# Token-shift mixing moved from the loaded RWKV blocks to the point where each projected block leaves PSUM

## What is computed

```python
shifted = jnp.pad(p_in, ((0, 0), (1, 0), (0, 0)))[:, :-1]
xl = p_in + (shifted - p_in) * mu
r, k, v, xw, xa, xg = jnp.split(xl, RWKV_SPLITS, axis=-1)
```

## Time and profile before

| | us |
|---|---|
| median of 3 runs | 2064.92 |
| lowest, highest | 2062.79, 2067.34 |
| profiled execution | 2061.17 |
| its span | 2059.4 |
| TensorE busy in the span | 1906.2 (93%) |
| VectorE busy | 859.3 (42%) |
| ScalarE busy | 426.5 (21%) |
| GpSimd busy | 1278.9 (62%) |

### The profile page before, as it was taken

How to read it: one execution, slowest core, us unless ns; L and a number is a source line. 1 busy time by engine, 2 the same in 40 slices (tenths; PEclk the granted TensorE clock), 3 DMA queues, 4 the chain that set the end, 5 groups by cost and what they waited for, 6 DMA issues and landing times.

```text
span 2059.4 us, 29817 instructions
## 1 busy us (share of the span) xinstructions
PE 1906.2 (93%) x11700; PEld 1482.6 (72%) x11700; DVE 859.3 (42%) x1426; ACT 426.5 (21%) x862; POOL 1278.9 (62%) x619
## 2 busy tenths in 40 slices
PE   7999999888779999999799989997868799999998
PEld 5888888656557888888477866676755678888887
DVE  4333321267664333311404244357756635555301
ACT  3000000123431000000213145534431021111100
POOL 6888877734066888877375442333364667777773
PEclk9999999989989999999899999999968999999999
DMA  4222223311022222233242421140023222223231
GB/s 149 92 92 98 93 86 94 118 35 59 11 82 72 92 92 93 92 96 97 99 160 98 160 100 53 42 149 8 4 109 112 72 82 92 92 92 93 91 95 59
DMA packets 58780, 180.33 MB, mean 88 GB/s; under 512 B 6931, under 2 KB 13843, under 8 KB 58172
## 3 DMA queue, kind: packets, MB, share of 16 engines
q1 hardware_dynamic: 49132, 165.83, 24.0%
q10 hardware_dynamic: 9552, 13.13, 1.8%
HBM read 165.81 MB, written 13.13 MB: 87 GB/s over the span
## 4 chain that ended last, share of the span: by engine, by line
PE 82%; DVE 12%; ACT 3%; issue 2%; DMA 0%; ACTq 0%; POOL 0%; DVEq 0%; SPq 0%; POOLq 0%
PE bank L531 23%; PE bank L533 23%; PE bank L532 23%; PE bank L893 1%; DVE h_lo L1643 1%; PE bank L846 1%; PE bank L581 1%; PE bank L879 1%; DVE xT L1690 1%; DVE tmp L1687 1%; DVE sq L2205 1%; PE bank L810 1%; DVE m_lo L2206 1%; DVE sq L2202 1%; PE bank L1051 1%
## 5 line engine op out<-in xcount | busy, mean ns | idle before, releaser
L444 POOL TENSOR_TENSOR w_hi<-w_raw,one 128x1024 fp32r<-128x1024 f32 (+1 forms) x279 | 527.1, 1889 | 595.1 <-PE bank L533 584.0
L446 POOL TENSOR_TENSOR w_lo<-w_raw,w_hi 128x1024 fp32r<-128x1024 f32 (+1 forms) x279 | 696.4, 2496 | 21.9
L531 PE MATMUL bank<-h_hi,w_hi 128*128 128x512 f32 x1528 | 628.1, 411 | 26.6 <-DVE h_lo L1643 12.5
L532 PE MATMUL bank<-h_lo,w_hi 128*128 128x512 f32 x1528 | 606.8, 397 | 0.0
L533 PE MATMUL bank<-h_hi,w_lo 128*128 128x512 f32 x1528 | 606.5, 397 | 0.0
L531 PEld LDWEIGHTS bank<-h_hi,w_hi 128*128 128x128 f32 x1528 | 288.8, 189 | 119.5 <-issue 27.9
L532 PEld LDWEIGHTS bank<-h_lo,w_hi 128*128 128x128 f32 x1528 | 289.3, 189 | 76.0 <-issue 9.8
L533 PEld LDWEIGHTS bank<-h_hi,w_lo 128*128 128x128 f32 x1528 | 288.8, 189 | 70.5
L531 PE MATMUL bank<-a_hi,w_hi 128*128 128x512 f32 x528 | 208.6, 395 | 0.0
L532 PE MATMUL bank<-a_lo,w_hi 128*128 128x512 f32 x528 | 208.6, 395 | 0.0
L533 PE MATMUL bank<-a_hi,w_lo 128*128 128x512 f32 x528 | 208.6, 395 | 0.0
(11 more groups left out here) (342 smaller groups left out, 2116.0 us busy)
## 6 DMA issues: line engine op xcount, KB each, us to landing
w_raw<-w_ffn_gu_dram SPq DMA_DIRECT2D x88, 512.0 KB, 3.4
w_raw<-w_conv_up_dram SPq DMA_DIRECT2D x44, 512.0 KB, 3.5
w_raw<-w_ffn_down_dram SPq DMA_DIRECT2D x32, 448.0 KB, 3.2
w_raw<-w_ffn_down_dram SPq DMA_DIRECT2D x16, 512.0 KB, 3.5
w_raw<-w_out_dram SPq DMA_DIRECT2D x16, 512.0 KB, 3.5
w_raw<-w_gates_dram SPq DMA_DIRECT2D x16, 512.0 KB, 3.5
w_raw<-w_rwkv_dram SPq DMA_DIRECT2D x14, 512.0 KB, 3.4
w_raw<-w_conv_down_dram SPq DMA_DIRECT2D x16, 448.0 KB, 3.3
```

The costliest lines, as they stand in the source:

```text
L444: nc.gpsimd.tensor_tensor(w_hi[:, s, 0:width], raw, one[:, 0:1].to_broadcast([P, width]), ALU.mult).then_inc(sem("w_rounded"), 1)
L446: nc.gpsimd.tensor_tensor(w_lo[:, s, 0:width], raw, w_hi[:, s, 0:width].bitcast(F32), ALU.subtract).then_inc(sem("w_split"), 1)
L531: nc.tensor.matmul(dst, hi, rhs_hi[:, k, :], start=start and k == k0, stop=False)
L532: nc.tensor.matmul(dst, hi, rhs_lo[:, k, :], start=False, stop=False)
```

## The change

The mix moves to where a block leaves PSUM. For each of the 14 RWKV blocks:

- ScalarE's copy now multiplies by 1 - mu, a column of the new tile `stay`, that VectorE makes once.
- VectorE then adds mu times the block shifted by one token, read from the same bank, in one instruction over 511 tokens (`mix_shifted`). Only this one now returns the bank to TensorE (`fill_read`).
- ScalarE's DMA of block f is issued by `send(f)` at the start of block f + 1's turn, after a wait for VectorE.
- The 14 `mix_shifted` stand at fixed places in VectorE's order in the attention's preparation: one behind each head's scaling, one more, two behind the four kd products, and six around the two compressions; the last stands ahead of the first attention unit's masks.
- `mix` and its 14 calls are gone. Readers of `pin` wait for the load alone.

The blocks in DRAM are now mixed ones. Nothing else changes.

```diff
--- before.py
+++ after.py
@@ -163,6 +163,7 @@
         head_ones2, eye2 = rcs[:, 6 * C:6 * C + P], rcs[:, 6 * C + P:]
         w2a2 = sb("w2a2", [P, 4 * P])
         PC = sb("PC", [P, 4, NCH])
+        stay = sb("stay", [P, 14])
         keep = sb("keep", [P, 4])
         psum = ctx.enter_context(nc.psum_tensor("bank", [P, 8, S], F32))
         bank = [psum[:, i, :] for i in range(8)]
@@ -1372,9 +1373,19 @@
             logs()
             filled = [0]
 
+            def send(f):
+
+                late = f - NFILL + LATE
+                act.wait_ge(*nth("fill_read", f + 1))
+                act.dma_start(fill_dram.ap()[:, f * S:(f + 1) * S],
+                              stage[:, f % 8, :] if late < 0 else late_stage[:, late, :])\
+                    .then_inc(sem("fill_late" if late >= 0 else f"fill_out{f // 4 % 2}"), 16)
+
             def fill_out(n=1):
 
                 for f in range(filled[0], filled[0] + n):
+                    if 1 <= f <= 14:
+                        send(f - 1)
                     act.wait_ge(*nth("w_used", FIRST["rwkv"] + f + 1))
                     late = f - NFILL + LATE
                     if f == 0:
@@ -1382,10 +1393,16 @@
                     elif f >= 8 and f % 4 == 0 and late < 0:
                         act.wait_ge(*nth(f"fill_out{f // 4 % 2}", 64 * (f // 8)))
                     place = stage[:, f % 8, :] if late < 0 else late_stage[:, late, :]
-                    nc.scalar.activation(place, bank[fill_bank(f)][:, :], ACT.Copy).then_inc(sem("fill_read"), 1)
-                    act.wait_ge(*nth("fill_read", f + 1))
-                    act.dma_start(fill_dram.ap()[:, f * S:(f + 1) * S], place)\
-                        .then_inc(sem("fill_late" if late >= 0 else f"fill_out{f // 4 % 2}"), 16)
+                    if f < 14:
+
+                        if f == 0:
+                            act.wait_ge(*nth("stay_ready", 1))
+                        c = RW_ORDER[f]
+                        nc.scalar.activation(place, bank[fill_bank(f)][:, :], ACT.Copy, scale=stay[:, c:c + 1])\
+                            .then_inc(sem("fill_scaled"), 1)
+                    else:
+                        nc.scalar.activation(place, bank[fill_bank(f)][:, :], ACT.Copy).then_inc(sem("fill_read"), 1)
+                        send(f)
                 filled[0] += n
 
 
@@ -1495,7 +1512,7 @@
                 act.wait_ge(*nth("keep_ready", 1))
                 nc.scalar.activation(MOD[:, :], RATE[m], ACT.Identity, bias=keep[:, m:m + 1], scale=param("k_a", m))\
                     .then_inc(sem("key_rate"), 1)
-                act.wait_ge(*nth("mixed_in", 3 * m + 5))
+                act.wait_ge(*nth(f"pin_in{m + 1}", 16))
                 if m:
                     act.wait_ge(*nth("rw_head_sum", 2 * m - 1))
                 nc.scalar.activation(sq[:, 0, :], pin[:, 4 + m, :], ACT.Square, scale=param("k_k", m))\
@@ -1518,7 +1535,7 @@
                     .then_inc(sem("kk_rstd"), 1)
 
             fill_out(2)
-            act.wait_ge(*nth("mixed_in", 2))
+            act.wait_ge(*nth("pin_in0", 16))
             nc.scalar.activation(pin[:, 13, :], pin[:, 13, :], ACT.Sigmoid)
             nc.scalar.activation(pin[0:64, 12, :], pin[0:64, 12, :], ACT.Tanh).then_inc(sem("lora_in"), 1)
             fill_out(1)
@@ -1876,6 +1893,15 @@
             pre_norm("nsa", "attn_norm", "nsa_h_ready")
             dve.wait_ge(*nth("nsa_small_in", 8 * 16))
             nc.vector.memset(rel[32:33, :], 1.0).then_inc(sem("rel_one"), 1)
+            nc.vector.tensor_scalar(stay[:, :], prm[:, COL["mu"]:COL["mu"] + 14], -1.0, 1.0, ALU.mult, ALU.add)\
+                .then_inc(sem("stay_ready"), 1)
+
+            def mix_shifted(f):
+
+                place, c = stage[:, f % 8, :], RW_ORDER[f]
+                dve.wait_ge(*nth("fill_scaled", f + 1))
+                nc.vector.scalar_tensor_tensor(place[:, 1:], bank[fill_bank(f)][:, 0:S - 1], param("mu", c),
+                                               place[:, 1:], ALU.mult, ALU.add).then_inc(sem("fill_read"), 1)
             job = [0]
 
             def job_bank():
@@ -1910,15 +1936,21 @@
                 dve.wait_ge(*nth("head_rstd", i + 1))
                 nc.vector.tensor_tensor(zn[:, i, :], zn[:, i, :], tmp[:, i, :], ALU.mult)\
                     .then_inc(sem("head_rstd_used"), 1)
+                if i:
+                    mix_shifted(i - 1)
             for i in range(2, 6):
                 dve.wait_ge(*nth("head_rstd", i + 1))
                 nc.vector.scalar_tensor_tensor(reverse(qn[:, i - 2, :]), by_tile(zn[:, i + 4, :]), param("q_norm"),
                                                by_tile(tmp[:, i % 2, :]),
                                                ALU.mult, ALU.mult).then_inc(sem("head_rstd_used"), 1)
+                mix_shifted(i - 1)
+            mix_shifted(5)
             for c in range(4):
 
                 nc.vector.tensor_scalar(kd[:, c, :], job_bank()[:, :], param("k_norm"), -HD ** -0.5, ALU.mult,
                                         ALU.mult).then_inc(sem("nsa_read"), 1)
+            mix_shifted(6)
+            mix_shifted(7)
             chain = [0]
 
             def link(ins):
@@ -1936,6 +1968,9 @@
                 link(nc.vector.tensor_tensor(t, x, x, ALU.mult))
                 link(nc.vector.scalar_tensor_tensor(t, t, 0.044715, x, ALU.mult, ALU.mult))
                 nc.vector.tensor_tensor(t, t, x, ALU.add).then_inc(sem("gelu_arg"), 1)
+                mix_shifted(8 if v == 0 else 11)
+                if v == 0:
+                    mix_shifted(9)
                 dve.wait_ge(*nth("gelu_tanh", v + 1))
                 link(nc.vector.scalar_tensor_tensor(t, t, 1.0, x, ALU.add, ALU.mult))
                 nc.vector.tensor_scalar(x, t, 0.5, None, ALU.mult).then_inc(sem("gelu"), 1)
@@ -1946,9 +1981,12 @@
                     link(nc.vector.tensor_tensor(kcn[:, :], kcn[:, :], tmp[:, 0, 0:w], ALU.mult))
                     nc.vector.tensor_scalar(kcn[:, :], kcn[:, :], param("k_norm"), -HD ** -0.5, ALU.mult, ALU.mult)\
                         .then_inc(sem("kc_normed"), 1)
+                    mix_shifted(10)
                 else:
                     nc.vector.tensor_copy(vct[:, :, :].rearrange("n g d -> n (g d)"), job_bank()[0:NCMP, 0:2 * HD])\
                         .then_inc(sem("nsa_read"), 1)
+                    mix_shifted(12)
+                    mix_shifted(13)
             dve.wait_ge(*nth("toeplitz_in", 16))
 
             def nsa_mask(n, g, unit):
@@ -2014,20 +2052,6 @@
                 ins.then_inc(sem("rw_step"), 1)
                 dve.wait_ge(*nth("rw_step", steps[0]))
 
-            def mix(j):
-
-                for i, (a, _) in enumerate(RW_GROUPS):
-                    if j == a:
-                        dve.wait_ge(*nth(f"pin_in{i}", 16))
-                if j:
-                    dve.wait_ge(*nth("mixed_in", j))
-                c = RW_ORDER[j]
-                x, d = pin[:, c, :], tmp[:, 1, :]
-                nc.vector.tensor_scalar(d[:, 0:1], x[:, 0:1], -1.0, None, ALU.mult)
-                link(nc.vector.tensor_tensor(d[:, 1:], x[:, 0:S - 1], x[:, 1:], ALU.subtract))
-                nc.vector.scalar_tensor_tensor(x, d, param("mu", c), x, ALU.mult, ALU.add)\
-                    .then_inc(sem("mixed_in"), 1)
-
             def decay_sum(m):
 
                 dve.wait_ge(*nth("lora_read", m + 1))
@@ -2038,7 +2062,7 @@
 
                 MOD = pair_sets[m % 2][1]
                 dve.wait_ge(*nth("key_rate", m + 1))
-                dve.wait_ge(*nth("mixed_in", 3 * m + 5))
+                dve.wait_ge(*nth(f"pin_in{m + 1}", 16))
                 link(nc.vector.tensor_tensor(MOD[:, :], MOD[:, :], pin[:, 4 + m, :], ALU.mult))
                 nc.vector.scalar_tensor_tensor(sq[:, 1, :], pin[:, m, :], param("r_k", m), MOD[:, :], ALU.mult,
                                                ALU.mult).then_inc(sem("rk_product"), 1)
@@ -2089,16 +2113,12 @@
 
             nc.vector.tensor_scalar(keep[:, :], prm[:, COL["k_a"]:COL["k_a"] + 4], -1.0, 1.0, ALU.mult, ALU.add)\
                 .then_inc(sem("keep_ready"), 1)
-            for j in range(5):
-                mix(j)
+            dve.wait_ge(*nth("pin_in0", 16))
             nc.vector.memset(decay[:, :, 0:1], 1.0)
             decay_sum(0)
             keys(0)
-            mix(5)
             decayed(0)
-            mix(6)
             sums_out(0)
-            mix(7)
             removal(0)
             replacement(0)
             keys(1)
@@ -2132,8 +2152,6 @@
                             .then_inc(sem("level_x_read"), 1)
                         if half == 0 and k > 1:
                             level_dt_out(m, k - 1)
-                    if m < 2 and k < 4:
-                        mix(7 + 3 * m + k)
                     if m < 3 and k < 5:
                         (sums_out, decay_sum, decayed, removal)[k - 1](m + 1)
                 level_dt_out(m, 5)
```

## The result

| | before | after |
|---|---|---|
| median, us | 2064.91 | 2012.87 |
| lowest, highest | 2062.79, 2067.34 | 2012.34, 2013.52 |
| span of the profiled execution | 2059.4 | 2010.8 |

The ratio is 0.9748, with a 95% interval of 0.9731 to 0.9765: 52 us faster, where 12.4 had been forecast.

The account below looks back on a forecast made before the run. TensorE held 82% of the chain that ended last, VectorE 12%. Terms -7.9 + 0 + 1.1 - 5.6 = -12.4 us took the median from 2064.92 to 2052.5 us, range 2048.5 to 2060.5.

Parts of the forecast that it names:

- (d): Rival: level-loop mixes worth their full 9.7 us, attention gain kept: -14.2, 2050.7 us, or 2049.6 with cw1 on time; chance 0.08.
- Step 1, initial mixes: Before the first RWKV level loop: removing eight mixes only lengthens VectorE's idle 12.55 us, worth 0.
- Step 1, level loops: RWKV level loops 0 and 1: removing three mixes in each gains 7.9 us, bounds 3.5 to 9.7.
- Step 2, copy and shifted add: Fills: ScalarE's scaled copy (0.78 us) and VectorE's multiply-add (0.75 us) fit in 1.0 us of slack; cost 0, at most 4 x 0.75.
- Step 3, the second load of cmp_w1: ScalarE's queue: cw1's DMA issued 3.2 us late behind a send, copy, table load and Tanh; cost 1.1 us, bounds 0 to 3.2.
- Step 4, the first attention unit: VectorE's eight multiplications of E slip ahead of GpSimd's split, ending TensorE's 4.71 us stall; gain 5.6 us, bounds 0 to 5.6.
- (a): Rival: in the first attention unit GpSimd's split still gets in, no gain there: -6.8, 2058.1 us; chance 0.22.
- (b): Rival: mixes only half on the level loops' path, 3.5 us gained, no attention gain: -2.4, 2062.5 us; chance 0.10.
- (c): Rival: banks come back too late, so every fill waits, 19 us in all: +12.2, 2077 us; chance 0.05.

Follow-up runs that it names:

- pad64: The kernel before the change with one unused 64-byte tile per partition ahead of `keep`, no instruction differing: 2025.12 us, ratio 0.9797.
- after_unmoved: The changed kernel with its new 56-byte tile `stay` at the end of memory, every other tile where it lay before the change: 2051.72 us, ratio 0.9935.
- unmoved_late: after_unmoved plus one useless 0.75 us VectorE instruction ahead of the eight multiplications of E in the first attention unit: 2055.71 us, ratio 0.9941.

## Why the prediction was wrong, and where it was right

**The step that failed** is in the first part: "The change lives between about 1100 and 1460 us of the span". The prediction costed instructions and waits, and took the added tile for nothing. That tile moved the matmuls' operands by 64 bytes against their weights. The 6168 large matmuls then start every 0.2267 us instead of every 0.2333, and this is 39 of the 52 us (pad64: 2025.12 against 2064.14). No rival held it either, (d) least of all. The new tile stands in the diff ahead of tiles that TensorE reads all the time; no row of before could have told the sign or the size, but that all of the kernel's 6168 large matmuls depend on where these tiles begin could have been a rival, and the range was as wide as the costs that were listed and no wider.

**The sum itself** can be tested on after_unmoved, where only the code differs. It was -12.4, and the medians give 2051.72 - 2064.14 = -12.4; the interval of the ratio reaches from -17 to -10. The terms, from the stages of the two profiled executions:

- Step 1, initial mixes: worth 0 was forecast; `keep` to the first `mats` is 77.56 in both. Right.
- Step 1, level loops: -7.9 forecast, -8.4 from the stages (bounds 3.5 to 9.7). Putting the mixes back cost 9.1 in the same two loops. By the prediction's own measure, second X copy to last DT copy, loops 0 and 1 take 1409.70 - 1396.61 = 13.1 and 1437.64 - 1424.56 = 13.1 us, where the earlier trace rows give 16.62 and 17.46. The prediction names 13.1 and 13.6; its own sum needs 13.1 for both, and 13.1 it was.
- Step 2, copy and shifted add: 0 forecast. The changed kernel's instructions by source line (ns, min/median/max):

```profile
L1903 DVE SCALAR_TENSOR_TENSOR stage<-bank,prm,stage x14: 728/742/751, 1086.5 to 1166.1; 128x511 f32<-128x511 f32 x14
...
L1401 ACT ACTIVATE stage<-bank,stay x14: 670/687/690, 1075.8 to 1165.4; 128x512 f32<-128x512 f32 x14
```

  The 0.75 of VectorE was right, the copy takes 0.69 between the bounds of 0.60 and 0.78, and no fill starts late: the stage up to block 13 is 110.0 in both.
- Step 3, the second load of cmp_w1: +1.1 forecast (the prediction's own addends make 1.0), 0 found. From ScalarE and its queue in after_unmoved, and TensorE's use:

```profile
1161.01 0.69 ACT L1401 ACTIVATE stage<-bank,stay 128x512 f32<-128x512 f32 x1 [10.57 <-DVE stage L1903]
1161.09 0.46 ACTq L1436 DMA_DIRECT2D cw<-cmp_w_dram  x1
1161.72 1.28 ACT L1432 ACT_TABLE_LOAD   x1
...
1163.01 0.31 ACT L1432 ACTIVATE hid<-hid 128x124 f32<-128x124 f32 x1
...
1170.36 7.31 PE L811 MATMUL bank<-zn,cw 128*128 128x62 f32 x64
```

  The DMA stands behind block 9's copy, the table load and the Tanh in the program, but is issued at 1161.09, 0.08 after the copy's start and ahead of both others. Nothing it waits for was late, so of the 3.2 us only the mix and the send count. Against the transposes of zn, which stand 0.51 earlier in this execution, it is 1161.09 + 0.51 - 1160.52 = 1.1 late; it lands 8.5 later at 1169.6, before TensorE asks at 1170.36. The mis-sized term is the 2.1 us of copy and table load that I put ahead of the DMA. The Tanh did come late, by 1163.01 + 0.51 - 1160.52 = 3.0, but VectorE ends the gelu at 1163.90 and TensorE takes it up at 1164.15, close to where it stood before (1164.69, less the 0.51).
- Step 4, the first attention unit: -5.6 forecast, -5.8 found, and undone by 0.75 us of other work. Of the 5.6, 4.2 is the earlier start of TensorE's next fill and 1.4 the clock: in before the fill behind the wait of 4.71 runs from 1206.31 to the split at 1213.64, 7.33 us with a granted clock of 0.50 in 1205 to 1208, against 5.94 for the fill ahead of it. In after_unmoved the fill behind the wait of 0.16 runs from 1201.37 to the split at 1207.31, 5.94 us at a granted clock of 1.00. The margin, from the start of the last multiplication to the split, was 0.31 us where the prediction put 0.25. The later masks lengthen TensorE's first wait from 0.27 to 1.12, by 0.85, where 0.96 was forecast.
- The order of VectorE and GpSimd decides between 1.66 and 5.54 us for the same eight instructions (after_unmoved, unmoved_late). In before VectorE's fourth starts 0.06 after the split and takes 2.01, until the split is over, where one undisturbed takes 0.28. The table load ahead of the exponentials costs its own 1.28 us alone: in after_unmoved it ends at 1191.70 and the exponential starts at 1191.71.

Of the rivals, (a) falls with step 4, (b) with the level loops, and (c) with the stage up to block 13. (d) had the loops at their full 9.7; they gave 8.4. That the terms found add up to (d)'s -14.2 all the same is chance: cw1 on time and the attention make up for it.

The terms give -14.2, the spans of the two profiled executions -12.0 (2047.4 against 2059.4). Most of the difference is the merge stage, 2.7 longer in after_unmoved. There one and the same instruction of VectorE is short or long while GpSimd splits weights beside it, as in these two rows of before:

```profile
1595.90 2.78 DVE L2206 TENSOR_TENSOR m_lo<-sq,m_hi 128x512 fp32r<-128x512 f32 x1
1604.18 0.69 DVE L2206 TENSOR_TENSOR m_lo<-sq,m_hi 128x512 fp32r<-128x512 f32 x1
```

How many are long differs from run to run (that the split is the reason was not tried here). The stage took between 56.9 and 59.6 us in the nineteen profiles, whatever was changed, and before's 56.9 is the lowest of them. So the exact agreement of -12.4 is partly luck. In the profiled execution of the changed kernel the stage up to block 13 has another such piece, a clock of 0.93 from 1075 to 1095 us, which pad64 does not have (110.0 against 108.4).

## What to carry to other kernels

A new tile can move others: before a difference is put down to the code, compare the start-to-start time of the commonest matmul in a stage that the edit doesn't touch. Where TensorE bounds a kernel of 128x512 fp32r matmuls that each load their weights, place the moving operands a multiple of 256 bytes from the weights, or try a pad of 32 to 224 bytes; here 64 bytes took the start-to-start time from 0.2333 to 0.2267 us and were worth 39 us, three times the edit's own worth. And an order between VectorE and GpSimd that holds by 0.2 to 0.3 us is a gain that the next edit may lose, as 0.75 us of other work did here.

## What the runs showed of the hardware that I had not expected

- The start-to-start time of 128x512 fp32r matmuls depends on the distance in bytes between the moving operand and the weights: 0.2267 us at a multiple of 256, 0.2289 at 64, 0.2333 to 0.2343 at the other steps of 32. Their own places, as far as these runs moved them, don't matter. Why is open.
- ScalarE's queue issued a DMA 1.9 us ahead of the Tanh that stands before it in the program, beside a running copy and ahead of a table load.
- 1.4 us of useless work on VectorE made the kernel 4.6 us faster, and 0.75 us of it elsewhere made the attention of another 6.0 us longer.
